# A second, converting load in place of ScalarE's rounding of weight chunks in a two-layer transformer kernel

## Reference, cut to what matters

```python
def rmsnorm(t, g):
    tf = t.astype(jnp.float32)
    y = tf * lax.rsqrt(jnp.mean(tf * tf, axis=-1, keepdims=True) + EPS)
    return (y * g.astype(jnp.float32)).astype(t.dtype)
...
    qk, v, o, z, i_pre, f_pre, mq, mz = split_cols(
        h @ w_in, [2 * M_WIDTH, M_WIDTH, M_WIDTH, M_WIDTH, M_HEADS, M_HEADS, MEM_WIDTH, MEM_WIDTH])
...
    x = x + jnp.square(jax.nn.relu(hm @ w_up[l])) @ w_down[l]
```

## Time and profile before

| | |
|---|---|
| median of 3 runs | 1576.82 us (1575.44 to 1581.01) |
| profiled execution, its own time | 1579.46 us |
| its span, first to last instruction | 1577.7 us |
| mean granted TensorE clock | 0.991 |
| PE busy | 1531.7 us, 97% of the span |
| DVE busy | 890.2 us, 56% |
| ACT busy | 715.3 us, 45% |
| POOL busy | 223.5 us, 14% |
| DMA queue of SyncE and ScalarE loads (q1) | 139.55 MB, 29.3% of 16 engines |

### The profile page before, as it was taken

How to read it: one execution, slowest core, us unless ns; L and a number is a source line. 1 busy time by engine, 2 the same in 40 slices (tenths; PEclk the granted TensorE clock), 3 DMA queues, 4 the chain that set the end, 5 groups by cost and what they waited for, 6 DMA issues and landing times.

```text
span 1577.7 us, 19176 instructions
## 1 busy us (share of the span) xinstructions
PE 1531.7 (97%) x7086; PEld 1239.6 (79%) x7086; DVE 890.2 (56%) x1753; ACT 715.3 (45%) x1630; POOL 223.5 (14%) x194
## 2 busy tenths in 40 slices
PE   7998999999999999999899999999999999999998
PEld 5886777877898777777587878788777888888886
DVE  6467485657565566666457557664455444434344
ACT  6553343334355667665335354442344433324243
POOL 3203020202120003122022005220001100000001
PEclk9999999999999999999999999999999999999999
DMA  6522121323424221112133312134323333333332
GB/s 194 161 68 80 54 80 55 107 68 120 119 76 147 77 61 56 54 56 67 41 121 94 94 55 67 56 109 131 93 81 94 94 93 96 105 94 93 97 103 81
DMA packets 88636, 141.56 MB, mean 90 GB/s; under 512 B 6368, under 2 KB 36448, under 8 KB 88544
## 3 DMA queue, kind: packets, MB, share of 16 engines
q1 hardware_dynamic: 87824, 139.55, 29.3%
q10 hardware_dynamic: 720, 0.80, 0.2%
HBM read 138.23 MB, written 2.10 MB: 89 GB/s over the span
## 4 chain that ended last, share of the span: by engine, by line
PE 79%; DVE 8%; ACT 5%; issue 3%; POOL 3%; DMA 2%; SPq 0%; ACTq 0%; POOLq 0%; DVEq 0%
PE banks L1259 12%; PE banks L1261 12%; PE banks L1260 12%; PE banks L1264 10%; PE banks L1266 10%; PE banks L1265 10%; PE banks L1222 3%; DVE sb_w_split L1964 3%; ACT sb_junk L1529 2%; DVE sb_arena L1973 2%; PE banks L1437 1%; PE banks L1384 1%; ACT sb_w_split L1561 1%; PE banks L1500 1%; DVE sb_arena L1964 1%
## 5 line engine op out<-in xcount | busy, mean ns | idle before, releaser
L1964 DVE TENSOR_TENSOR sb_w_split<-sb_raw,sb_w_split 128x512 fp32r<-128x512 f32 (+4 forms) x530 | 345.0, 693 | 365.9 <-ACT sb_w_split L1561 365.5
L1561 ACT ACTIVATE sb_w_split<-sb_raw 128x512 fp32r<-128x512 f32 (+4 forms) x530 | 288.1, 592 | 411.2 <-PE banks L1261 192.0
L1259 PE MATMUL banks<-sb_actA,sb_w_split 128*128 128x512 f32 x672 | 277.1, 412 | 2.8 <-DVE sb_arena L1964 2.5
L1261 PE MATMUL banks<-sb_actA,sb_w_split 128*128 128x512 f32 x672 | 263.0, 391 | 0.0
L1260 PE MATMUL banks<-sb_actA,sb_w_split 128*128 128x512 f32 x672 | 262.1, 390 | 0.0
L1264 PE MATMUL banks<-sb_w_split,sb_actB 128*128 128x512 f32 (+2 forms) x464 | 181.4, 391 | 1.6 <-DVE sb_w_split L1964 1.6
L1266 PE MATMUL banks<-sb_w_split,sb_actB 128*128 128x512 f32 (+2 forms) x464 | 175.9, 379 | 0.0
L1265 PE MATMUL banks<-sb_w_split,sb_actB 128*128 128x512 f32 (+2 forms) x464 | 175.5, 378 | 0.0
L1264 PE MATMUL banks<-sb_w_split,sb_actA 128*128 128x512 f32 (+1 forms) x384 | 154.4, 402 | 13.5 <-DVE sb_w_split L1964 9.6
L1259 PEld LDWEIGHTS banks<-sb_actA,sb_w_split 128*128 128x128 f32 x672 | 126.5, 188 | 32.7 <-issue 7.1
L1266 PE MATMUL banks<-sb_w_split,sb_actA 128*128 128x512 f32 (+1 forms) x384 | 150.3, 391 | 0.0
(11 more groups left out here) (226 smaller groups left out, 2188.2 us busy)
## 6 DMA issues: line engine op xcount, KB each, us to landing
sb_raw<-in_a_w_in SPq DMA_DIRECT2D x66, 256.0 KB, 3.0
sb_raw<-in_w_up SPq DMA_DIRECT2D x32, 512.0 KB, 3.8
sb_raw<-in_w_down SPq DMA_DIRECT2D x32, 512.0 KB, 3.8
sb_raw<-in_w_in SPq DMA_DIRECT2D x24, 512.0 KB, 3.7
sb_raw<-in_mem_w_kv SPq DMA_DIRECT2D x16, 512.0 KB, 3.8
sb_raw<-in_w_ckv SPq DMA_DIRECT2D x16, 512.0 KB, 3.8
sb_raw<-in_a_w_in SPq DMA_DIRECT2D x15, 512.0 KB, 3.7
sb_raw<-in_a_w_out SPq DMA_DIRECT2D x12, 512.0 KB, 3.9
```

The lines of the kernel that those rows point to most:

```text
L1259: pe.op.matmul(out, hi[:, cs], x.hi(k), start=i == 0, stop=False)
L1261: t = pe.op.matmul(out, lo[:, cs], x.hi(k), start=False, stop=last_i)
L1561: act.op.activation(hi[:, cs], raw[:, cs], ACT.Copy).then_inc(act.mark(m("w_hi"), 2 * n + part + 1), 1)
L1964: dve.op.tensor_tensor(out, a, b, op).then_inc(dve.mark(*mark) if mark else dve.tick(), 1)
```

## The change

The rounded part no longer comes from ScalarE. GpSimd issues a DMA of its own for each chunk that reads the same weights from HBM a second time and converts them to fp32r on the way into `sb_w_split`. ScalarE's `split` step is gone. DVE's `split` waits once, for both loads, instead of for each half of the rounding. GpSimd's new step stands in the list where ScalarE's stood, and waits for the slot of chunk n-3 as that one did. The first wait of GpSimd, for the constants, is moved behind its first loads.

```diff
@@ scalar_program
-        if kind == "split":
-            n = a[0]
-            name, c = plan.chunks[n]
-            raw, hi, _, _ = v.chunk(n, name, c)
-            act.wait_ge(m(f"dma_raw{n % RAW_SLOTS}"), m.raw_total(n))
-            if n >= SPLIT_SLOTS:
-                act.wait_ge(*m.chunk_done(n - SPLIT_SLOTS))
-            half = raw.shape[-1] // 2
-            for part in range(2):
-                cs = slice(part * half, (part + 1) * half)
-                act.op.activation(hi[:, cs], raw[:, cs], ACT.Copy).then_inc(act.mark(m("w_hi"), 2 * n + part + 1), 1)
-        elif kind == "enter":
+        if kind == "enter":
@@ vector_program
             half = raw.shape[-1] // 2
+            dve.wait_ge(m(f"dma_raw{n % RAW_SLOTS}"), m.raw_total(n))
+            dve.wait_ge(m(f"dma_hi{n % SPLIT_SLOTS}"), m.raw_total(n, SPLIT_SLOTS))
             for part in range(2):
                 cs = slice(part * half, (part + 1) * half)
-                dve.wait_ge(m("w_hi"), 2 * n + part + 1)
                 tensor(lo[:, cs], raw[:, cs], hi[:, cs].bitcast(F32), ALU.subtract, m("w_lo"), 2 * n + part + 1)
@@ new function
+def weight_parts(v, n, name, c, home):
+
+    pr = PRODUCTS[name]
+    k0, kk = pr.order[c]
+    w = v.io[pr.w[0]][pr.w[1]] if len(pr.w) > 1 else v.io[pr.w[0]]
+    rows = slice(pr.k0 + k0 * P, pr.k0 + (k0 + kk) * P)
+    home, at, found = home.rearrange("p (k n) -> p k n", k=kk), 0, []
+    for c0, width in pr.parts:
+        found.append((home[:, :, at:at + width], w[rows, c0:c0 + width].rearrange("(k p) n -> p k n", p=P)))
+        at += width
+    return found
@@ gpsimd_program
-    pool.wait_ge(m("dma_cons"), 16)
+    const_read = False
     for step in plan.order:
         kind, a = step[0], step[1:]
+        if kind == "split":
+            n = a[0]
+            name, c = plan.chunks[n]
+            if n >= SPLIT_SLOTS:
+                pool.wait_ge(*m.chunk_done(n - SPLIT_SLOTS))
+            for out, src in weight_parts(v, n, name, c, v.chunk(n, name, c)[1]):
+                pool.op.dma_start(out, src).then_inc(m(f"dma_hi{n % SPLIT_SLOTS}"), 16)
+            continue
+        if not const_read:
+            pool.wait_ge(m("dma_cons"), 16)
+            const_read = True
```

More of the change, by code:

```diff
@@ L1172, in chunk_done, with raw_total @@
         return self(f"full{bank}" if kind == "full" else "chunk"), value
-    def raw_total(self, n):
-        return 16 * sum(len(PRODUCTS[self.plan.chunks[m][0]].parts) for m in range(n % RAW_SLOTS, n + 1, RAW_SLOTS))
+    def raw_total(self, n, slots=RAW_SLOTS):
+        return 16 * sum(len(PRODUCTS[self.plan.chunks[m][0]].parts) for m in range(n % slots, n + 1, slots))
 class Stream:
@@ L2617, in sync_program @@
             name, c = plan.chunks[n]
[L2618 to L2621, removed]
             if n >= RAW_SLOTS:
                 sp.wait_ge(m("w_lo"), 2 * (n - RAW_SLOTS) + 2)
[L2624 to L2628, removed]
+            for out, src in weight_parts(v, n, name, c, v.chunk(n, name, c)[0]):
+                sp.op.dma_start(out, src).then_inc(m(f"dma_raw{n % RAW_SLOTS}"), 16)
         elif kind == "gate_loads":
```

## The result

The changed kernel takes 1824.8 us in the median (1813.9 to 1836.8, 4 runs), the kernel before 1576.1: a ratio of 1.157 (95% interval 1.150 to 1.165), 249 us slower. The forecast was 1718. The mechanism forecast is in the trace, and so are two that had been priced at almost nothing.

What follows compares the result with a forecast made beforehand. PE was taken as the bound, busy 97% of the span. Terms 70 + 3.5 + 18 + 9 + 42 + 3 + 4 + 2 - 10 = +141.5 on 1579.5 gave 1721, as median 1718 us; 8-in-10 range 1605 to 1860.

Steps and rivals of the forecast that it cites:

- DVE held ahead of its evictions: At 37 product boundaries, 15 in the MLP, `lo` 4.5 us late delays evictions: 1.9 us each, +70 us.
- The issue by GpSimd: For each chunk's second load, GpSimd's issue was taken as 1.00 us, with bounds 0.38 and 2.90.
- GpSimd's own work: At the pooling windows two loads stand behind GpSimd's work, +3 us; the norms' powers waiting behind slots add nothing.
- Start and memory tokens: Start: one more MB loaded, +2 us; 32 memory-token chunks at +0.55 a load, +18, and two boundaries without slack, +9.
- Attention and softmax: At 14 hand-overs where PE already waits for DVE evictions, 3 us more each: +42 us, bounds 0 and 160.
- The tail: Last chunk: `lo` 4.5 us late against 0.5 us of slack, +4 us.
- ScalarE's freed time: Outside the MLP, PE waits where ACT's other work stood behind a rounding are given back: -10 us.
- C: Rival: the load is quick, 3.3 to 4 us after the slot is free; 1610 us, 1590 to 1640; chance 0.14.
- D: Rival: faster, `lo` starts under 3.3 us after the free slot, no boundary stalls; 1550 to 1565 us; chance 0.04.
- E: Rival: nothing changes, boundary stalls and what ScalarE gives back cancel; within 8 us of 1577; chance 0.04.
- B: Rival: second load much dearer, `lo` 8 us or more after the free slot; 1915 us; chance 0.16.
- A: The forecast: DVE held by the second load, 4 to 6 us after the free slot; 1650 to 1800 us; chance 0.62.

Runs made afterwards that it cites:

- the later `lo`: Changed kernel with DVE's `lo` step one chunk later, behind the evictions: 1656.7 us; the same edit on the kernel before, ScalarE rounding: 1626.0 us.
- the busy run: Changed kernel with ScalarE doing scratch work of the size and in the place of the removed rounding: 1841.0 us, ratio 1.169.
- the SyncE run: Changed kernel with the second load issued by SyncE as a plain, unconverted load, output not the reference's: 1683.8 us, ratio 1.068.
- the run with four slots: Kernel before with the change for the last 60 chunks only, four `hi` slots, each load issued one chunk earlier: 1580.4 us, ratio 1.002.

## Why the prediction was right, point by point

**DVE held ahead of its evictions: right in place and size.** Forecast were 1.9 us at each of 15 MLP boundaries; from the start of a product's last matmul to the start of the next product's first, they grew by 29.4 us in all, 2.0 each. At the 22 boundaries before they grew by 33.4 where 41.8 stood in the sum. The way to `lo` was put at 5.2 us: 0.4 until the issue and 4.4 to 4.7 to the landing are 4.8 to 5.1, with single ones up to 6.0 (1567.35 to 1573.39). The landing was the better guess from rows than the rule: the Trainium skill ("DMA: Bandwidth & Descriptors", "Anatomy of one DMA — SWDGE (gpsimd) path") makes it an estimated 3.2 us. The measurement decides; by the rule the MLP would have lost almost nothing, and it lost 38.

**The issue by GpSimd:** 1.0 us was taken, 0.72 measured. No sign that DVE held it up: the median issue is 0.72 us with DVE busy and with DVE idle (all lie between 0.56 and 0.83). Of the Trainium skill's warning ("SBUF — State Buffer", "SBUF: two separate sides") no run here shows anything.

**GpSimd's own work: the step that failed.** The sum had +3 for it, at the pooling windows, where it cost 18.5; and it said that the norms' powers could be passed over, since "PE must have come to those anyway". That looked at loads that hold up powers and not at powers and sums that hold up loads. The order had shown the load behind the window in so many words; the same reading was not made for the 28 powers and the 38 square sums. 46 late issues, some 195 us late in sum, are the result; moving the issue to SyncE won 117 us outside the MLP, and that is what they and the slower way to `lo` cost there together.

**Start and memory tokens: mis-sized.** Up to `mzA` the stage lost 28 us, where +2 and some +5 stood. With the later `lo`, going over to the second load costs 22 (66.1 to 88.3), and SyncE's issues win back only 4 (82.7). PE's first matmul comes at 12.84 us, for 7.96. One thing there was misread: the change is described as moving GpSimd's wait for the constants behind its first loads, but the list of steps begins with a load of `x`, and the wait stands at that first step.

```profile
6.97 1.30 POOL L2502 DMA_DIRECT2D sb_w_split<-in_a_w_in  x2 [6.55 <-DMA sb_cons<-in_cons]
```

What it cost isn't shown: SyncE issues the first one at 3.09 us, without that wait, and DVE's first `lo` still comes at 10.34, for 10.86 here. The DMA engines are 0.96 busy from 3 to 11 us, so there the loads may hold each other up; from 11 to 20 us they are 0.68 busy, and how the rest of the stage divides between late issues and traffic is open. Rounding the first 17 chunks by ScalarE won back 15 us of the whole. The eight products on memory tokens, each to the start of the next product, took 48 us more in all (161 for 113), 12.5 of them in the start; 18 and 9 stood in the sum, and with SyncE's issues it is 22.

**Attention and softmax: too dear.** +42 stood for it, and the attention stage grew by 22.6 us (162.3 to 184.9). The 14 waits of the rows were read as 1 to 2 us each and as the attention's; they are 0.2 to 2.2 us, and six of them, 6.1 us, lie in that stage. This surplus hid part of what was missing elsewhere. The tail (+4, measured 3.9) and ScalarE's freed time (-10, measured 16 by the busy run) were near.

**The clock: left out.** The text had expected no fall at stalls of 2 us, and named a fall as a sign of being wrong. In the MLP it fell at two hand-overs, behind PE stalls of 2.4 us (ending at 1423.7) and 2.0 us (1477.5), and not at the others, of 1.2 to 2.9 us; so the size of the stall alone doesn't tell. Elsewhere it fell some 30 times, around stalls of 1 to 13 us. The mean grant fell from 0.991 to 0.954, and 7086 matmuls took 1601.6 us for 1531.7. These 70 us are a cost of the idle time, not a cause beside it: they are 34 in the SyncE run (1565.8) and 21 with the later `lo` (1552.5).

**The rivals.** C, D and E are out. Of B, the dearer load, only the total is as near as A's (1915 is 90 us off, 1718 is 107): the single landing was as in A. The chance of 0.92 for slower and the range to 1860 held because the range took in B's lower part, not because its mechanism came.

## What to carry to other kernels

A wait moved from one engine to another is worth what stands behind it in the new queue: list what the waiting engine has behind it (here DVE's evictions), and what the issuing engine has ahead of it (here GpSimd's sums, powers and windows), step by step for every kind of work it does. A load released by the same event as the work that it replaces is late by its whole landing; it wants a slot more, and then costs almost nothing (1580.4 for 1618.7 us, with 1577.5 before). Before an engine with work of its own gets to issue loads, count its waits for others: each of them is now a wait of the loads.

## What the runs showed of the hardware that was not expected

A converting load from GpSimd of 512 KB took 4.4 to 4.7 us from issue to landing in the MLP (medians), the plain one from GpSimd 4.5 to 4.7. In the run in which SyncE issued both, the one issued first took 3.8 and the raw one behind it 4.7; in the run with four slots, GpSimd's took 4.1 to 4.3 and SyncE's raw ones 4.5 and 4.6. So the difference between the engines is not told apart from the order and the overlap of the two. 60 more loads of 512 KB under full matmuls changed nothing of the total (ratio 0.999) but lengthened SyncE's from 3.8 to 4.5 and 4.8 us.
